# Order of two quarter loads among the seven products of a feed-forward layer

## The reference

```python
D_FF = 2816
def swiglu(x, w_gate, w_up, w_down):
    return (jax.nn.silu(x @ w_gate) * (x @ w_up)) @ w_down

for l in range(DEPTH):                      # DEPTH = 2
    x = layer_norm(ALPHA * x + 0.5 * swiglu(x, ffn1_w_gate[l], ffn1_w_up[l], ffn1_w_down[l]), ...)
    ...                                     # the mixer
    x = layer_norm(ALPHA * x + 0.5 * swiglu(x, ffn2_w_gate[l], ffn2_w_up[l], ffn2_w_down[l]), ...)
```

## Time and profile before

| | |
|---|---|
| median of 3 runs | 2957.13 us (2955.15 to 2959.99) |
| time of the profiled execution | 2963.7 us |
| its span | 2961.8 us |
| mean granted TensorE clock | 0.992 |
| PE busy with matmuls | 2855.8 us (96%) |
| DVE busy | 1594.2 us (54%) |
| ACT busy | 1094.6 us (37%) |
| chain that ended last | PE 80%, DVE 10%, ACT 4%, DMA 4%, issue 2% |

### The profile page before, as it was taken

How to read it: one execution, slowest core, us unless ns; L and a number is a source line. 1 busy time by engine, 2 the same in 40 slices (tenths; PEclk the granted TensorE clock), 3 DMA queues, 4 the chain that set the end, 5 groups by cost and what they waited for, 6 DMA issues and landing times.

```text
span 2961.8 us, 34169 instructions
## 1 busy us (share of the span) xinstructions
PE 2855.8 (96%) x14401; PEld 2375.5 (80%) x14401; DVE 1594.2 (54%) x2211; ACT 1094.6 (37%) x1416; POOL 118.8 (4%) x123
## 2 busy tenths in 40 slices
PE   7999998999999989999999999999999999999998
PEld 7888877887887878878876878888888886788886
DVE  4345357734535665453556574635745364656455
ACT  4322443432234333232545432324323354543332
POOL 0020000001000000000100000000000010000000
PEclk9999999999999999999999999999999999999999
DMA  5242122323221223443521343423534351234342
GB/s 217 72 128 84 59 77 80 98 71 114 72 86 57 72 90 115 145 117 111 102 100 38 107 127 128 131 97 114 143 114 131 111 102 58 73 113 142 110 132 86
DMA packets 67816, 305.19 MB, mean 103 GB/s; under 512 B 6916, under 2 KB 7106, under 8 KB 40016
## 3 DMA queue, kind: packets, MB, share of 16 engines
q1 hardware_dynamic: 53216, 263.21, 26.1%
q0 software_dynamic: 12992, 32.00, 5.7%
q10 hardware_dynamic: 1456, 7.80, 0.9%
HBM read 294.60 MB, written 2.10 MB: 100 GB/s over the span
## 4 chain that ended last, share of the span: by engine, by line
PE 80%; DVE 10%; ACT 4%; DMA 4%; issue 2%; ACTq 0%; SPq 0%; DVEq 0%; POOLq 0%
PE G L483 14%; PE G L485 14%; PE G L484 14%; PE G L495 7%; PE G L497 7%; PE G L496 7%; DMA raw<-in_stream 3%; DVE w_lo L1675 2%; PE G L957 2%; PE G L959 2%; PE G L958 2%; ACT w_hi L1118 1%; PE A L1008 1%; PE A L1030 1%; PE A L670 1%
## 5 line engine op out<-in xcount | busy, mean ns | idle before, releaser
L483 PE MATMUL G<-xT_hi,w_hi 128*128 128x512 f32 (+1 forms) x2368 | 880.8, 372 | 17.7 <-DVE x L2232 6.0
L485 PE MATMUL G<-xT_hi,w_lo 128*128 128x512 f32 (+1 forms) x2368 | 869.7, 367 | 0.0
L484 PE MATMUL G<-xT_lo,w_hi 128*128 128x512 f32 (+1 forms) x2368 | 869.2, 367 | 0.0
L1675 DVE TENSOR_TENSOR w_lo<-raw,w_hi 128x2048 fp32r<-128x2048 f32 (+1 forms) x218 | 497.9, 2284 | 495.5 <-ACT w_hi L1118 495.2
L1118 ACT ACTIVATE w_hi<-raw 128x2048 fp32r<-128x2048 f32 (+1 forms) x218 | 413.2, 1896 | 696.4 <-PE G L485 366.2
L483 PEld LDWEIGHTS G<-xT_hi,w_hi 128*128 128x128 f32 x2368 | 448.8, 190 | 90.3 <-DVE x L2232 6.6
L485 PEld LDWEIGHTS G<-xT_hi,w_lo 128*128 128x128 f32 x2368 | 448.5, 189 | 73.3
L484 PEld LDWEIGHTS G<-xT_lo,w_hi 128*128 128x128 f32 x2368 | 449.1, 190 | 68.8
L495 PE MATMUL G<-w_hi,xT_hi 128*128 128x512 f32 (+1 forms) x512 | 193.3, 378 | 7.5 <-DVE xT_lo L2252 2.7
L497 PE MATMUL G<-w_hi,xT_lo 128*128 128x512 f32 (+1 forms) x512 | 186.1, 364 | 0.0
L496 PE MATMUL G<-w_lo,xT_hi 128*128 128x512 f32 (+1 forms) x512 | 185.9, 363 | 0.0
(11 more groups left out here) (315 smaller groups left out, 3651.7 us busy)
## 6 DMA issues: line engine op xcount, KB each, us to landing
raw<-in_stream SPq DMA_DIRECT2D x208, 1024.0 KB, 4.9
raw<-in_stream SPq DMA_DIRECT2D x80, 512.0 KB, 5.5
raw<-in_stream POOLq DMA_DIRECT2D x32, 512.0 KB, 9.7
lnr<-in_ln_rows POOLq DMA_DIRECT2D x6, 1024.0 KB, 5.2
row<-in_rows POOLq DMA_DIRECT2D x6, 512.0 KB, 7.1
x<-in_x ACTq DMA_DIRECT2D x1, 2048.0 KB, 17.9
tB<-fA ACTq DMA_DIRECT2D x4, 512.0 KB, 5.4
xn<-fB ACTq DMA_DIRECT2D x4, 512.0 KB, 8.4
```

The source lines that it names most:

```text
L483: mm(o, a, hi[:, c, at:at + n], start=start and own_start, stop=False, **k)
L484: mm(o, a, lo[:, c, at:at + n], start=False, stop=False, **k)
L485: return mm(o, wl[:, col:col + P], hi[:, c, at:at + n], start=False, stop=stop, **k)
L1675: tt(w_lo[:, s, 0:nk, :], raw[:, r, 0:nk, :], w_hi[:, s, 0:nk, :].bitcast(F32), ALU.subtract).then_inc(lo_done, 1)
```

## The change

SP loads W21 second-last and W12 last: W21 goes to `raw[0]` when product 0's low part is done, and W12 to `raw[1]` when product 1's low part is done. ACT, DVE and POOL follow: product 4 reads `raw[0]`, the third sum is made in `raw[1]` for product 5. With `taken(first + 4)` for `raw[0]`, the slot that the next part's first block takes is free one product earlier than before.

```diff
                     alternate(raw[:, 1], b + 2, 0, (half_in[1], raw_in[1]))
                     taken(first + 1)
                     slot_free()
-                    alternate(raw[:, 0], b + 2, 0, (half_in[0], raw_in[0]))
+                    alternate(raw[:, 0], b, 1, (half_in[0], raw_in[0]))
+                    taken(first + 4)
+                    slot_free()
+                    alternate(raw[:, 1], b + 2, 0, (half_in[1], raw_in[1]))
                     taken(first + 5)
-                    slot_free()
-                    alternate(raw[:, 1], b, 1, (half_in[1], raw_in[1]))
-                    taken(first + 4)
                     Q.split += PRODUCTS
                     b += 4
...
-                        act.wait_ge(half_in[1], 16 * (2 * N.parts + 2))
-                        act.wait_ge(raw_in[1], ((2 * Pos.pair + Pos.off - 2 - Pos.fewer) // 2 + 1) * 16)
+                        act.wait_ge(half_in[0], 16 * (2 * N.parts + 2))
+                        act.wait_ge(raw_in[0], ((2 * Pos.pair + Pos.off - 2 - Pos.fewer) // 2 + 1) * 16)
+                        split_summed(raw[:, 0])
+                        act.wait_ge(t3_sum, 32 * (N.parts + 1))
                         split_summed(raw[:, 1])
-                        act.wait_ge(t3_sum, 32 * (N.parts + 1))
-                        split_summed(raw[:, 0])
                         act.wait_ge(t4_sum, 32 * (N.parts + 1))
...
                         read_product(2, n)
+                        split_summed(raw[:, 0])
+                        read_product(3, n)
                         split_summed(raw[:, 1])
-                        read_product(3, n)
-                        split_summed(raw[:, 0])
                         read_product(4, n)
...
-                pool.wait_ge(half_in[0], 32 * p + 32)
-                pool.wait_ge(raw_in[0], (ring // 2 + 2) * 16)
-                add_from(raw[:, 0], b + 2, 1, t3_sum)
+                pool.wait_ge(half_in[1], 32 * p + 32)
+                pool.wait_ge(raw_in[1], (ring // 2 + 2) * 16)
+                add_from(raw[:, 1], b + 2, 1, t3_sum)
                 pool.wait_ge(lo_done, split + 5)
                 add_from(raw2[:, 0], b, 1, t4_sum)
```

## The result

The changed kernel takes 2965.74 us (median of 14 runs, 2961.58 to 2971.26) against 2958.53 us (14 runs, 2954.69 to 2961.36). The ratio is 1.0024, 95% interval 1.0017 to 1.0031: **slower by 0.24%, 7 us**, where +1.1% was forecast. One repeated run of the kernel before, at 5807 us, is counted as slow and stands in no comparison of this text. The profiled execution of the changed kernel is its fastest (2961.58 us, span 2959.7 us); that of the kernel before (2963.7 us) lies above all 14 of its runs. The two spans therefore differ by -2.1 us and say nothing of the sign. What the traces can tell is where the seven products lose time.

The account below looks back on a forecast made before the run. PE bounds the kernel, with matmuls under way in 96% of the span. Per part 3.7 + 1.6 us lost less 1.3 regained, 4.0 net, gives +32 us over eight parts: median 2957.13 becomes 2989 us, +1.1%, range 2953 to 3003.

Parts of the forecast that it names:

- 3.7 + 1.6 lost: Before product 6 in each part: a PE gap of 3.7 us, then 1.6 us lost to a lower granted clock.
- W21 first: At product 4: W21, issued earlier, lands in time and ACT's wait is gone, -10.5 us over eight parts.
- W12 second: At product 5: the third sum is issued 8.3 us later but lands at 1195.2, before its need at 1196.4, no wait.
- The fourth sum just in time if undisturbed: At product 6: undisturbed, the fourth sum lands at 1200.7 to 1202.1, say 1201.4, and is wanted at 1201.8.
- The slot freed earlier disturbs it: Next part's blocks move beside the fourth sum: the first costs 2.7 us, the second up to 2.4; landing 1205.7, 3.9 late.
- The sum: Per part 3.7 + 1.6 lost, 1.3 regained, 4.0 net; over eight parts +32 us.
- B: Rival, about even: only the first block delays the fourth sum, landing 1203 to 1204.1, time 2955 to 2963; chance 0.2.
- A: Rival, faster: the blocks don't slow the fourth sum, the 10.5 us are gained, 2947 us; chance 0.12.
- C: Rival, much slower: the third sum is late too, product 5 waits, say, 2 us, gaps add, 3013 us; chance 0.1.
- D: Rival: a DMA takes 2.0 us plus bytes / 436e3, both sums land by 1194, A holds; no chance beyond A's.
- The rule of the Trainium skill: Engines alternate between software and hardware queues, so the fourth sum is late; were sums served first, it would not be.

Follow-up runs that it names:

- the repeat: The changed kernel measured again with no edit, against the kernel before: 2967.46 us, ratio 1.0013 (1.0002 to 1.0024).
- two versions without any loss: The changed kernel with the next part's first block loaded after product 5's low part (0.9986, again 0.9988), and the changed kernel without the fourth sum (0.9982), against the kernel before.
- the late block: The changed kernel, but SP loads the next part's first block only after product 5's low part: 2957.86 and 2957.43 us, 0.9986 and 0.9988 to the kernel before.

## Why the prediction was wrong

The sign was right, and so was where the wait goes and which load causes it; the size was not: +32 us forecast, +7 measured (+4 in the repeat). **The step that failed is "3.7 + 1.6 lost"**, the gap and the clock that followed from a landing worked out by turns with both blocks. The runs showed a gap of 1.2 us on average (9.4 us over eight parts), no loss of clock, and nothing taken by the second block. By its own steps:

- **W21 first: the wait at product 4 is gone.** Right in all traces of the changed kernel. Its worth was mis-sized: 10.5 us were read from one execution. Four traces give 5.2 on average by the longer measure, and two versions without any loss come to -3 to -5 us. "All that W21's lateness costs" was said of the kernel and is true only of that execution. A hint was in the numbers: its 2963.7 us lay above all three runs then known. This error works the other way: with 5.2 in place of 10.5 the forecast would have been +37.
- **W12 second: the third sum 8.3 us later, without a wait.** Right. Issued at 1186.01 (forecast 1186.2), landed at 23.7 to 25.6 (forecast 24.0), product 5 not delayed but once, by 0.5 us.
- **The fourth sum just in time if undisturbed.** Right: forecast 29.5 to 30.9, measured 28.5 to 30.6 with the late block.
- **The slot freed earlier disturbs it.** Right in kind, and this is the term of the sum that was mis-sized most. Landing 34.5 was forecast, 31.9 measured. Of the 2.6 us between them 0.6 are the undisturbed landing (30.2 taken, 29.6 measured), 0.4 the first block (2.7 charged, 2.3 measured) and 1.6 the second (1.6 charged in the end, nothing gained where it was held back). The first block's figure is near by luck: it was charged all of its own time, as if it met the sum from its issue on, and met only the last 81 packets. A row of before could have warned of it: W21's load in the earlier trace rows took 9.5 to 12.2 us beside the third sum, which itself was hardly late., from which the turns were read, show two queues of 4 and 8 KB runs, neither an accumulating one, and not what happens right behind an issue.
- **3.7 us of gap and 1.6 of clock per part.** Wrong by what came before it: 1.04 in part 1, 1.67 at most, no clock. Forecast loss of the changed kernel 42 us, measured 9.4. The clock's part isn't settled by the length of the gap: of the gaps in the eight parts, over all traces, none up to 1.7 us had a spell of low clock behind it, 1.8, 1.9 and 2.0 had one, 2.1 and 2.8 had none, and 4.4, the only one of the length forecast, had one (0.59).
- **The sum** with the measured terms is 9.4 - 5.2 = +4.2 us. The 7.2 of the first comparison is 3 more: the interval of the repeat (+0.6 to +7) holds 4.2, that of the first comparison (+5 to +9) doesn't. Outside the eight parts the traces scatter from 2732.8 to 2742.8 us, spells of low clock included (before 2735.0 on average in four, after 2738.5 in three), and the run without the fourth sum has 2742.2 there without any gap in the parts. The three traces with 2740 us or more there have a mean granted clock of 0.989 to 0.991, the others 0.991 to 0.993. Whether the change has a part in that is open; with so few traces it can't be told from chance.
- **The rivals.** B, "only the first block gets between, or only in part", is what happened: landing 1203.3 in part 1 (1203 to 1204.1 by B), a gap of 1.04 (1.0 to 2.1), the clock kept. It put the time at 2955 to 2963, and the measured one is nearly 3 us above this, as B too subtracted 10.5. A, C and D didn't occur. D had both sums there by 1194; the halves landed 6.1 to 15.1 us behind their issues, the last at 1203.3. The rule of the Trainium skill ("DMA: Bandwidth & Descriptors", section "SWDGE vs HWDGE vs iDMA": the engine goes round-robin between the queues) isn't what the first 3 us behind the issue show, 320 packets to none. Behind that it agrees with the trace of the kernel before, 179 packets of the sum and 199 of W21's load.

The version with the early W21 and the late block beats both kernels, by 0.12 to 0.14% against the one before: below what counts as a difference here by my bound of 0.2%, though both intervals lie under 1.

## What to carry to other kernels

When a reordering frees a slot early, ask what the load that it triggers runs into: a megabyte that nobody waited for cost the whole gain and more, and holding it back with one changed number gave the gain. A load that must run beside a transfer on the critical path can be harmless in another form (here two DMAs in runs of 2 KB for one in runs of 8 KB). And before pricing a wait that hangs on DMA timing, look at more than one trace: the same kernel lost 11.0, 2.0, 3.6 and 4.1 us in the same eight places. To price a load beside another transfer, count what is left of that transfer when the load's first packet moves, here some 3.5 us behind its issue, and not when it is issued.

## What was not expected of the hardware

- An ordinary load issued behind queued accumulating DMAs moved nothing for 3.4 to 3.7 us (1.0 with none queued), however much of the accumulating transfer was left; W21's load in the kernel before, with half a sum left, did the same. Then the load pushed past the last packets (90 to 38). It landed after 8.2 us instead of 4.7.
- Beside the end of an accumulating DMA, 1 MB in runs of 8 KB delayed it by 2.1 us on average (7.9 us over eight parts), the same amount as two DMAs in runs of 2 KB by 0.2 us (0.2 us).
- Two such megabytes delayed it by 3.0 us on average, from 29.6 to 32.6, hardly more than one (2.3), but up to 35.3.
- Gaps of PE of 1.8, 1.9 and 2.0 us were followed by a low granted clock (0.57 to 0.63 over 4 us), gaps of 2.1 and 2.8 were not.
